# Output projection in three rounded passes with the decode rows last, four feed-forward groups issued behind it, and three levels of a recurrence in one PSUM tile

## The reference

```python
b = jnp.cumsum(gc, axis=2)                      # recurrence, per head and chunk of rows
att = jnp.einsum('bhtk,bhtsk,bhsk->bhts', qc, exp(b_t - b_s), kc)   # s <= t
o = einsum(qc * exp(b), s) + einsum(att, vc)    # and the state s goes on to the next chunk
mix = (mg_a * y_a + mg_b * y_b) @ lw['w_out']
x1 = _ln_affine(DN_ALPHA * x + gt_m * mix, lw['ln1_g'], lw['ln1_b'])
h2 = _ln_plain(x1) * (1.0 + sc_f) + sh_f
f_out = (gelu(conv3(h2 @ w_up)) * (h2 @ w_gate)) @ w_down
x2 = _ln_affine(DN_ALPHA * x1 + gt_f * f_out, lw['ln2_g'], lw['ln2_b'])
```

## Time and profile before

| | |
|---|---|
| median of 3 runs | 2513.82 us (2513.56 to 2517.86) |
| the profiled execution | 2512.13 us, span 2510.3 us, mean granted TensorE clock 0.950 |
| PE busy | 2266.3 us, 90% of the span |
| DVE, ACT, POOL busy | 959.3, 644.1, 695.3 us |
| from the end of the merge products to the first feed-forward product | 178 us |
| from the first feed-forward product to the end | 778 us |

### The profile page before, as it was taken

How to read it: one execution, slowest core, us unless ns; L and a number is a source line. 1 busy time by engine, 2 the same in 40 slices (tenths; PEclk the granted TensorE clock), 3 DMA queues, 4 the chain that set the end, 5 groups by cost and what they waited for, 6 DMA issues and landing times. The chain is left out here.

```text
span 2510.3 us, 34681 instructions
## 1 busy us (share of the span) xinstructions
PE 2266.3 (90%) x14458; PEld 1953.4 (78%) x14458; DVE 959.3 (38%) x1865; ACT 644.1 (26%) x1315; POOL 695.3 (28%) x419
## 2 busy tenths in 40 slices
PE   3996999996898979986799999995999999999997
PEld 2994777863676769986699998445999898998996
DVE  6004333123666630249831043452332232322327
ACT  2102222121565631223422220032222121121213
POOL 3203222010111122214421210353443342332426
PEclk8997999876999989998999999997999999999998
DMA  6545343135200041100122111213211111110202
GB/s 217 191 126 216 132 150 130 64 145 166 98 27 29 2 119 51 34 9 2 53 62 91 34 51 68 92 60 122 57 54 40 37 57 45 51 51 26 71 23 87
DMA packets 136612, 197.08 MB, mean 79 GB/s; under 512 B 15217, under 2 KB 105259, under 8 KB 131726
## 3 DMA queue, kind: packets, MB, share of 16 engines
q1 hardware_dynamic: 128043, 150.47, 18.7%
q0 software_dynamic: 8368, 44.12, 5.0%
q10 hardware_dynamic: 44, 0.27, 0.0%
HBM read 172.74 MB, written 26.36 MB: 79 GB/s over the span
## 5 line engine op out<-in xcount | busy, mean ns | idle before, releaser
L2676 PE MATMUL PS<-part_hi,w_ff_hi 128*128 128x344 f32 x1056 | 339.2, 321 | 0.0
L2676 PE MATMUL PS<-part_hi,w_ff_lo 128*128 128x344 f32 x1056 | 337.4, 320 | 0.0
L2676 PE MATMUL PS<-part_lo,w_ff_hi 128*128 128x344 f32 x1056 | 337.4, 319 | 0.0
L2676 PEld LDWEIGHTS PS<-part_hi,w_ff_hi 128*128 128x128 f32 x1056 | 199.1, 189 | 6.2 <-issue 5.8
L2676 PEld LDWEIGHTS PS<-part_hi,w_ff_lo 128*128 128x128 f32 x1056 | 198.8, 188 | 0.0
L2676 PEld LDWEIGHTS PS<-part_lo,w_ff_hi 128*128 128x128 f32 x1056 | 198.5, 188 | 0.3
L2798 POOL TENSOR_TENSOR w_ff_lo<-w_raw,w_ff_hi 128x1024 fp32r<-128x1024 f32 x44 | 105.6, 2401 | 299.6 <-ACT w_ff_hi L2749 299.6
L2855 DVE TENSOR_SCALAR conv_sb<-up_sb,conv_wT 128x1024 f32<-128x1024 f32 x22 | 41.9, 1905 | 292.7 <-ACT up_dec L2765 292.7
L478 PE MATMUL PS<-h_hi,w_hg_parts 128*128 128x344 f32 x576 | 139.0, 324 | 8.4 <-DMA part_lo<-h_lo_rows 8.4
L1583 ACT ACTIVATE scores<-scores,mins_p 128x640 f32<-128x640 f32 (+5 forms) x192 | 112.9, 590 | 122.5 <-DVE mins_p L1620 122.5
L2713 PE MATMUL PS<-w_down_hi,act_hi 128*128 128x512 f32 x352 | 139.4, 396 | 0.0
(11 more groups left out here) (474 smaller groups left out, 4760.5 us busy)
## 6 DMA issues: line engine op xcount, KB each, us to landing
w_or_ada<-w_ada SPq DMA_DIRECT2D x8, 2048.0 KB, 7.8
w_raw<-w_up SPq DMA_DIRECT2D x22, 512.0 KB, 5.1
w_raw<-w_gate SPq DMA_DIRECT2D x22, 512.0 KB, 4.2
w_raw<-w_down SPq DMA_DIRECT2D x22, 512.0 KB, 3.7
w_ada_sb<-w_ada SPq DMA_DIRECT2D x4, 2048.0 KB, 22.2
w_hg_raw<-w_in SPq DMA_DIRECT2D x16, 512.0 KB, 3.5
w_merge_raw<-w_in SPq DMA_DIRECT2D x16, 512.0 KB, 3.9
h_hi_rows<-h_hi SPq DMA_DIRECT2D x1, 4128.0 KB, 15.0
```

The lines of the kernel that those rows point to most:

```text
L2676: last = pe.matmul(PS[:, e % BANKS, 0:cols], r(wt[:, s, k, :]), r(ht[:, k, t0:t0 + cols]), start=k + i == 0, stop=k == KD - 1 and i == 2)
```

## The change

In the recurrence, levels 0, 1 and 2 are computed as 8, 16 and 32 small products of 64, 32 and 16 rows and columns and land in disjoint places of one PSUM pair, so that one `pick` takes all three (6 picks a head instead of 8). The differences of level 0 go: ACT makes its decays directly by 16 exponentials of 64 columns with a bias a chunk, one half from `lf`, one from its negated middle row `nref`. The PSUM ring is counted by U, seven a head.

`w_out` is loaded in `hgrn_and_merge` during the branch products, ACT rounds its eight slices and POOL subtracts their low parts there, into memory that becomes free slice by slice. `output_projection` splits `mix` into a high and a low part (ACT and DVE) and multiplies in three rounded passes of 512 columns, 24 products for half a tile. The transposes of tile s-2 stand between the halves of tile s. The decode rows are multiplied in float32, with four products of 256 columns in four column groups of the array. The convolution weights and states are prepared in this block behind tile 0; x is loaded into the tile's own buffer; `z` has one buffer; ACT modulates and POOL lowers one tile behind instead of two, and the first up and gate weights are loaded and split behind tiles 2 and 3. In the last tile DVE scales and shifts the upper half, POOL the lower. At its end PE issues four groups of the feed-forward part (up and gate of slice 0, columns 0 to 687) between the last tiles. `ffn` then starts with their third pieces; the gate row is spread behind them, and it loads only one small constant before its weights. Buffers are at fixed addresses (`low`).

```diff
-    lev.append(s == t)
+    lev = [lev[0] | lev[1] | lev[2]] + lev[3:] + [s == t]
...
+                if u == NG + 1:
+                    sp.wait_ge(o_low, 6)
+                    for i in range(4):
+                        k = slice(2 * i, 2 * i + 2)
+                        sp.dma_start(wo_raw[:, k, :], a["w_out"][0].rearrange("(k p) n -> p k n", p=P)[:, k, :]).then_inc(wo_in[i], 16)
...
             for u in range(NU):
                 weights.low(pool, u, landed(u))
+                if u == NU - 2:
+                    out_low(0)
+                    out_low(1)
+            for n in range(2, KD):
+                out_low(n)
...
+                        U = 7 * h + max(w - 2, 0)
+                        if U >= 2 and w not in (1, 2):
+                            hh, uu = divmod(U - 2, 7)
+                            if uu == 6:
                                 pe.wait_ge(kdT_done, hh + 1)
...
+                            out = PS[:, 2 * (U % 2) + c // 4, P * (c % 4):P * (c % 4) + P]
+                            if w < 3:
+                                half = 64 >> w
+                                for b in range(1 << w):
+                                    r = slice(2 * half * b, 2 * half * b + half)
+                                    k0, q0 = P * c + r.start, P * c + r.stop
+                                    last = pe.matmul(out[r, r.stop:r.stop + half], X[:, n % 3, k0:k0 + half], X[:, n % 3, q0:q0 + half],
+                                                     start=True, stop=True)
+                            elif w == 8:
...
+                if w == 0:
+                    if J >= 3:
+                        products_done(act, J - 3)
+                    act.wait_ge(nref_ready, 1)
+                    for c in range(NT):
+                        k, q, middle = P * c, P * c + 64, P * c + 63
+                        act.activation(E[:, J % 3, k:k + 64], lf[:, h, k:k + 64], ACT.Exp, bias=lf[:, h, middle:middle + 1], scale=-1.0)
+                        last = act.activation(E[:, J % 3, q:q + 64], lf[:, h, q:q + 64], ACT.Exp, bias=nref[:, h, c:c + 1])
+                    last.then_inc(exp_done, 1)
...
             for u in range(NG, NU - 2):
                 weights.high(act, u + 2, landed(u + 2), (mm_done, 12 * (u - NG + 1)))
+                out_high(2 * (u - NG))
+                out_high(2 * (u - NG) + 1)
+            for n in range(4, KD):
+                out_high(n)
...
-            diff(0)
+            v.tensor_scalar(nref[:, :, :], lf[:, :, 0:L].rearrange("p h (c n) -> p h c n", n=P)[:, :, :, P // 2 - 1], -1.0, None, ALU.mult)\
+                .then_inc(nref_ready, 1)
             diff(1)
             multiply(0)
             for J in range(9 * (HH + 1)):
                 h, w = divmod(J, 9)
-                if J + 2 < jobs and (w + 2) % 9 != 7:
+                if J + 2 < jobs and (w + 2) % 9 not in (0, 7):
                     diff(J + 2)
                 if J + 1 < jobs and (w + 1) % 9 < LEV:
                     multiply(J + 1)
-                if h < HH and w < 8:
+                if h < HH and 2 <= w < 8:
...
+        tmp = raw[:, 2, :]
...
+            sp.wait_ge(mix_lo, len(seq) + 1)
+            for n, (name, f) in enumerate((("w_up", 0), ("w_gate", 0))):
+                src = a[name][0].rearrange("(k p) n -> p k n", p=P)[:, :, P * f:P * f + P]
+                sp.dma_start(raw[:, n, :].rearrange("p (k n) -> p k n", k=KD), src).then_inc(ff["raw_in"][n], 16)
...
+            def passes(s, k, c):
+                (hi, lo), (wh, wl) = (x[:, k, cols(s)] for x in (h2h, h2l)), (x[k][:, c] for x in (w_high, w_low))
+                return ((hi, wh), (hi, wl), (lo, wh))
+
+            def half_rows(s, half):
+                for k in range(KD):
+                    if half == 0 and k % 4 == 0:
+                        pe.wait_ge(mix_lo, s + 2 if s else k // 4 + 1)
+                    for i, (x_, w_) in enumerate(passes(s, k, slice(512 * half, 512 * half + 512))):
+                        last = pe.matmul(PS[:, pair(s) + half, :], r32(x_), r32(w_), start=k + i == 0, stop=k == KD - 1 and i == 2)
+                return last
+
+            def decode_rows(s):
+                pe.wait_ge(mix_lo, s + 2)
+                for k in range(KD):
+                    for i in range(3):
+                        for q in range(4):
+                            x_, w_ = passes(s, k, slice(DQ * q, DQ * q + DQ))[i]
+                            last = pe.matmul(PS[32 * q:32 * q + NB, pair(s), 0:DQ], x_, w_, start=k + i == 0, stop=k == KD - 1 and i == 2)
+                return last
+
+            def first_feed(kind, n):
+                if n == 0:
+                    pe.wait_ge(ff["lo_done"], kind + 1)
+                pe.wait_ge(h2_lo, (3, 6)[n])
+                for k in range(KD):
+                    hc = slice(T // 3 * n, T // 3 * n + T // 3)
+                    for i, (wt, ht) in enumerate(((wgh, h2h), (wgh, h2l), (wgl, h2h))):
+                        last = pe.matmul(PS[:, 2 * kind + n, 0:T // 3], r32(wt[:, kind, k, :]), r32(ht[:, k, hc]), start=k + i == 0, stop=k == KD - 1 and i == 2)
+                last.then_inc(ff["mm_done"], 1)
...
+            for s in range(len(seq)):
+                if s >= 2:
+                    pe.wait_ge(res_done, s - 1)
+                if s == DEC:
+                    transpose(s - 2)
+                    decode_rows(s).then_inc(mm_done, 1)
+                    continue
+                half_rows(s, 0)
+                if s >= 2:
+                    transpose(s - 2)
+                half_rows(s, 1).then_inc(mm_done, 1)
+                if s == 0:
+                    pe.wait_ge(one_in, 16)
+                    pe.wait_ge(gr_read, 1)
+                    for half in range(2):
+                        last = pe.matmul(PS[:, 6 + half, :], one[:, :], gr[:, 512 * half:512 * half + 512], start=True, stop=True)
+                    last.then_inc(gb_mm, 1)
+                    pe.wait_ge(k_in, 16 * 3)
+                    pe.transpose(PS[:, 4, 0:4 * FT], cwR[:, :], ident[0:4 * FT, 0:4 * FT])
+                    for f in range(FT):
+                        last = pe.transpose(PS[:, 5, 2 * NB * f:2 * NB * f + 2 * NB], old[:, P * f:P * f + P], ident[0:2 * NB, 0:2 * NB])
+                    last.then_inc(k_mm, 1)
+                if s == 1:
                     pe.wait_ge(gb_read, 1)
+            pe.wait_ge(res_done, LASTS)
+            first_feed(0, 0)
+            transpose(LASTS - 1)
+            first_feed(0, 1)
+            pe.wait_ge(res_done, LASTS + 1)
+            first_feed(1, 0)
+            transpose(LASTS)
+            first_feed(1, 1)
...
+            split_high(0, slice(0, 4))
+            split_high(0, slice(4, 8))
+            for s in range(1, len(seq)):
+                split_high(s, slice(0, KD))
+            for s in range(len(seq)):
+                deviation(s, sd, mv, stat_done, std_done)
+                deviation(s, sdb, mvb, stat2_done, std2_done)
+                if s >= 1:
+                    if s - 1 != DEC:
+                        modulate(s - 1)
+                    high(s - 1)
+                if s in (2, 3):
+                    feed_high(s - 2)
+            high(LASTS)
...
+                if s >= 1:
+                    lower(s - 1)
+                if s in (2, 3):
+                    feed_low(s - 2)
...
+            for s in range(len(seq)):
+                r, b = rows[s], s % 2
+                yt, tm = y[0:r, s % 3, :], tmp[0:r, :]
+                if s == DEC:
+                    for q in range(4):
+                        v.tensor_copy(tm[:, DQ * q:DQ * q + DQ], PS[32 * q:32 * q + NB, pair(s), 0:DQ]).then_inc(dec_moved, 1)
+                    v.wait_ge(dec_moved, 4)
+                    v.tensor_tensor(tm, tm, gr[0:NB, :], ALU.mult).then_inc(gated, 1)
+                else:
+                    v.tensor_tensor(tm, PS[:, pair(s):pair(s) + 2, :].rearrange("p a n -> p (a n)"), gB[:, :], ALU.mult).then_inc(gated, 1)
+                v.wait_ge(gated, s + 1)
+                v.scalar_tensor_tensor(yt, yt, ALPHA, tm, ALU.mult, ALU.add).then_inc(res_done, 1)
+                v.wait_ge(res_done, s + 1)
+                statistics(yt, st6[0:r, b], mv[0:r, b], stat_done)
+                normalize(yt, yt, mv[0:r, b], sd[0:r, b:b + 1], std_done, s + 1).then_inc(norm_done, 1)
+                if s == LASTS:
+                    v.wait_ge(norm_done, s + 1)
+                    v.tensor_tensor(yt[:, HI], yt[:, HI], g1[0:r, HI], ALU.mult).then_inc(high_scaled, 1)
+                    v.wait_ge(high_scaled, 1)
+                    v.tensor_tensor(yt[:, HI], yt[:, HI], b1[0:r, HI], ALU.add).then_inc(high_scaled, 1)
+                    v.wait_ge(high_scaled, 2)
+                v.wait_ge(scaled, s + 1)
+                statistics(yt, st6b[0:r, b], mvb[0:r, b], stat2_done)
+                if s:
+                    v.wait_ge(tr_done, s)
+                else:
+                    v.wait_ge(k_mm, 1)
```

(14 more changed lines are left out.)

426 lines of the change are left out of this document (222 added, 204 removed).

## The result

The changed kernel takes 2471.15 us (median of 4 runs, 2469.39 to 2473.45), the kernel before 2515.57 us (4 runs, 2513.56 to 2517.86): ratio 0.9824, 95% interval 0.9807 to 0.9841, 44 us faster. The prediction was 2471 us, range 2454 to 2487.

What follows compares the result with a forecast made beforehand. DVE bounds the recurrence, PE the tiles and feed-forward part, besides gaps; after the change the DVE-POOL chain sets the tiles. 2512.1 - 33.8 (output projection and feed-forward) - 9 (recurrence) = 2469.3, median 1.7 above: 2471 us, range 2454 to 2487.

Steps and rivals of the forecast that it cites:

- Recurrence: Recurrence stage: fewer masked copies and no level-0 differences, less exponentials, small products and collisions; -9 us (bounds -2, -15).
- the 1.0 us charged for small products: Recurrence, per head: PE's third job has 32 small products for 8, taken to cost 1 us a head.
- Start of the output projection: Block start: first product at 1557.9, 4.8 us earlier; DVE's chain starts at 1576.7, 20.1 us behind the block's first instruction.
- The 3.5 us charged for a low clock: Output projection start, tile 0: PE's low clock remains and costs 3.5 us (bounds 1.5, 5).
- Tiles 0 to 6: Output projection: the DVE-POOL chain sets tiles of 13.3, 13.85, or 16.1 us with weight splits; 100.35 us in all.
- One sign that was named: Output projection tiles: PE would wait before each transpose.
- Tile 7: Last full tile: decode rows, slowed by a fallen clock, end 16 us into it, 2 us after DVE is ready.
- Tail: Decode tile and block change: tile 8 starts at 1693.05, first feed-forward product at 1713.3; 20.25 us.
- Feed-forward: Feed-forward part: four groups fewer (15.1 us), less old low clock (1.4), plus gate row (1.75); -14.75 us.
- The rival of half clock: Output projection tiles: PE's clock falls while waiting on DVE; 22.5 us a tile, +66, 2537 us; chance 0.05.
- The rival of starvation: Feed-forward: PE reaches slice 1 before its weights, the 15.1 us come back; 2486 us; chance 0.07.
- The lighter chain: Rival: no POOL delay, cheaper splits, less clock loss at start and decode rows, full recurrence gain; 2458 us; chance 0.16.

## Why the prediction was right, and where only the sum was

The profiled execution was predicted at 2469.3 us and took 2469.39. Term by term, as measured less as predicted:

- **Stages ahead of the recurrence**: taken as unchanged, +2.7. This is the executions' own spread and no term of the change.
- **Recurrence**: -10.8 instead of -9, that is 1.8 better, and its two halves were both off. The exponentials: 0.24 us each was right (0.25 taken), and the delay of the first head was 2.9 us (some 2 taken). But the differences at a head's end, less the exponentials, gave 1.8 to 2.0 us a head and not 3.3. The packing was priced at less than nothing (1.0 for the copies, less 1.0 for small products, less 0.5 for collisions) and gave 1.4 to 2.8 a head. The failed step is the 1.0 us charged for small products: the 32 of the third job cost 0.73 us, against 2.0 for eight large ones, and where the prediction had a cost there was a gain, since DVE waits 0.2 to 1.3 us a head less for products. Copies less collisions, taken at 0.5, gave 0.9 to 1.5. Two errors of opposite sign met here, so the nearness of -9 and -10.8 is in part luck; the first head came 1.0 us later where 0.6 of gain was forecast.
- **Merge**: -0.8 instead of 0, the clock behind the recurrence, as the run with the old recurrence shows. The rounding of the projection's weights cost nothing, as predicted.
- **Start of the output projection**: the chain starts 17.24 us behind the block's first instruction, predicted 20.1. The 3.5 us charged for a low clock are the step that failed; the gate row and the small transposes took 0.6 more than their share. Products started 0.23 us apart from the second on, and the window has a clock of 0.97; before, the window with the wait for the weights had 0.70, and that wait is gone. The low clock came later, from 1564.2 to 1567.2 (0.50), behind 3.8 us in which PE was busy throughout with the gate row and the small transposes; there DVE set the tile and it cost nothing. Why it came there and not at the start is open. The executions differ here: where the block's first eight transposes ran at the low clock (1.87 us instead of 1.03), the chain started 18.2 us behind them; with the old recurrence it started 18.4 us behind although they took 1.03.
- **Tiles 0 to 6**: 99.7 instead of 100.35. The mechanism held to 0.2 us a tile: 13.3 for the chain, 13.75 where POOL's lowering delays the normalisation (13.85 taken), 15.9 where a weight slice stands ahead of the scale (16.1; the slice took 2.85 us beside the normalisation, and not 2.34 behind it, and ended 8.1 us into the tile instead of 8.3). One sign that was named did not appear: PE waits only from the transposes of tile 3 on; by then it had made up its late start into tile 1 (1564.2, at the low clock). The run with one product shows that PE had next to no part in it (the tiles shortened by 0.1 to 0.2 us), the one with the slices moved that those 2.15 us were the slices, and the one with the shared scale that POOL's 4.7 us were the part of the chain worth shortening. The normalisation took 1.29 us beside POOL's instruction, 0.81 alone. The Trainium skill, "SBUF — State Buffer", section "Who interferes with whom", has a `tensor_scalar` in a two-port mode and a GpSimd instruction exclude each other; the trace agrees.
- **Tile 7**: 14.1 instead of 16. PE did stand still for 7.07 us and came back at clock 0.50, but the low stretch was 4.8 us long, transposes included, and DVE waited 0.32 us for the decode rows where 2 were forecast. The mechanism was right and the size too large. Windows of PE alone in the changed kernel, around the decode rows:

```profile
1657.00:1664.90 7.90, 0.83 (x5) 0.87 0.16 66
1664.90:1669.70 4.80, 4.80 (x39) 0.50 0.01 3
1669.70:1678.70 9.00, 9.00 (x169) 1.00 0.15 59
```

- **Tail**: 24.1 instead of 20.25, the largest miss. Two things were left out: DVE's sum of 8 rows waits for POOL's lowering of tile 6 (3.29 us instead of 1.2), and the fourth early group stands behind transposes that come late, after 3.55 us without work, and so runs for 6.2 us at mostly half clock instead of 3.8. The run with the other order takes the second away, and with it the meeting of DVE's last lowering with POOL's, and gains 5.35. The first stands in it unchanged (3.35 us); no run takes it away. The prediction's addition for DVE is off as well: 1.4, 1.2, 1.2, 1.3, 0.2, 0.5 and 0.8 make 6.6 and not 6.9.
- **Feed-forward**: -13.3 instead of -14.75. Of the missing 1.45, some 0.5 are there by the third slice's gelu (63.24 us behind the first product, 77.46 before), and the gate row is half of them (2.0 us instead of 1.75); the other 0.9 grow evenly over the remaining 19 slices, some 0.04 a slice. They don't come from the early groups: with the groups in place every gelu from the third on lies 16.0 to 16.2 us later than in the changed kernel, and the same growth against the kernel before is there. What they are is open: the same products in the same order have the same median of 0.319 us in both traces. The 14.7 us of the run with the groups in place are another sum than the -14.75 of the prediction (16.1 less 1.4 of tail, within the changed kernel), and that the two agree is chance.

So the shape was right, and the total to a tenth of a microsecond was luck: terms of +2.7, -1.8, -0.8, -2.9, -0.6, -1.9, +3.9 and +1.45 cancel. The rival of half clock did not occur: the clock over the tiles was 0.95. With a third of the products it fell to 0.74 and the tiles did not lengthen, since PE had the time to lose; what 48 products a tile would do at that clock, no run shows. The rival of starvation did not occur. The lighter chain was partly so in the start and in tile 7, and the tail took it back.

## What to carry to other kernels

Work out the second engine's chain for a tile before making the first engine's part cheaper: here 2.5 us a tile were taken from TensorE and the tile shortened by 0.8 to 1.3, or grew by 1.3 where GpSimd was given a weight slice as well; the rest had to be fetched from the chain (a shared scale and shift, and side work moved into time in which GpSimd waited). At the end of a block look for an instruction that is ready but stands behind one that waits, on each engine. And when a change removes VectorE work by giving ScalarE small instructions, keep the old form where nothing runs beside them, as in the first head.

## What the runs showed of the hardware

- Two-input instructions of DVE were held until POOL's lowering was over, however small they were: 8x1024 in 3.29 us and 128x64 in 2.36 us beside it. Alone, 128x1024 of the first kind took 1.22 and 128x64 of the second 0.23. The Trainium skill, "SBUF — State Buffer", section "Who interferes with whom", says that a VectorE instruction with two SBUF inputs contends with GpSimd's reads; the trace agrees.
- A ScalarE activation of 64 columns with a bias column starts 0.24 us after the one ahead; one of 1024 columns without it takes 1.06 in all.
- Float32 products of 16 columns into column groups: 64 records in 0.73 us, against 16 records of 64 columns in 1.94, both at a granted clock of 0.50.
- TensorE's waits and the clock behind them, in the changed kernel: after 7.07 us it ran 4.8 us at clock 0.50, after 3.55 us some 5 us at the low level, after 2.96 us 4.1 us at 0.58; after 2.09 and 1.55 us the clock stayed at 1.00. The same kernel run again has the same picture (2.92 us with slow transposes behind it, 2.10 and 1.55 without).

```profile
1621.49 1.64 PE L2487 MATMUL PS<-ident,x_norm 128*128 128x128 f32 x8 [2.96 <-DVE x_norm L2637]
1621.40:1625.50 4.10, 4.01 (x15) 3.48 (x16) 3.89 (x6) 3.81 (x8) 1.20 (x1) 0.58 0.43 128
```

- A wait does not decide it alone: behind the same wait of 1.39 us, at the same place of two versions, the products started 0.285 us apart in one execution and 0.157 in the other.
- In the recurrence the granted clock fell from 0.90 to 0.75 and the stage got faster. Its copies wait for PE only 1.4 us in all there.
